# Prompt attention: a third PSUM bank for turned probabilities, one bank for the values of all branches

## What is computed

```
scale = HEAD_DIM ** -0.5
p_c = masked_softmax(jnp.einsum('bqghd,bngd->bghqn', qg, kc) * scale, mask_c)
o_c = jnp.einsum('bghqn,bngd->bqghd', p_c, vc)             # 32 compressed keys
...
p_s = masked_softmax(jnp.einsum('bqghd,bgqkd->bghqk', qg, kg) * scale, mask_s)
o_s = jnp.einsum('bghqk,bgqkd->bqghd', p_s, vg)            # selected keys; here all causal ones
...
p_w = masked_softmax(jnp.einsum('bqghd,blgd->bghql', qg, kw) * scale, mask_w)
o_w = jnp.einsum('bghql,blgd->bqghd', p_w, vw)             # window of 512 keys
o = g[:, :, 0] * o_c + g[:, :, 1] * o_s + g[:, :, 2] * o_w # sigmoid gates per head
```

## Time and profile before

| | |
|---|---|
| median of 3 runs | 1866.81 us (1864.55 to 1866.87) |
| the profiled execution | 1869.97 us, its span 1868.2 us |
| busy, whole span | PE 1665.7, PEld 1275.3, DVE 744.2, ACT 583.4, POOL 379.4 us |
| prompt attention | from 355 to 673 us of the span |

### The profile page before, as it was taken

How to read it: one execution, slowest core, us unless ns; L and a number is a source line. 1 busy time by engine, 2 the same in 40 slices (tenths; PEclk the granted TensorE clock), 3 DMA queues, 4 the chain that set the end, 5 groups by cost and what they waited for, 6 DMA issues and landing times. The chain is left out here.

```text
span 1868.2 us, 27344 instructions
## 1 busy us (share of the span) xinstructions
PE 1665.7 (89%) x11621; PEld 1275.3 (68%) x11621; DVE 744.2 (40%) x1232; ACT 583.4 (31%) x1097; POOL 379.4 (20%) x234
## 2 busy tenths in 40 slices
PE   4899898699989979999999849897999989997698
PEld 4345566466666669999977637784999965554375
DVE  2221111255455456660188734232321444444343
ACT  4001111255444443222245422334330402222221
POOL 1111000011000013322288724111120230000141
PEclk9999898799999999999999968998999989998699
DMA  9222253222111001111111153112000130002621
GB/s 335 67 78 46 84 140 89 73 93 91 46 47 47 2 16 46 46 46 35 27 35 35 57 151 146 57 49 85 24 24 24 35 102 1 23 23 79 228 91 62
DMA packets 120575, 129.93 MB, mean 70 GB/s; under 512 B 16728, under 2 KB 92938, under 8 KB 120326
## 3 DMA queue, kind: packets, MB, share of 16 engines
q1 hardware_dynamic: 120102, 128.08, 21.9%
q0 software_dynamic: 352, 0.10, 0.2%
HBM read 107.05 MB, written 23.18 MB: 70 GB/s over the span
## 5 line engine op out<-in xcount | busy, mean ns | idle before, releaser
L154 PE MATMUL banks<-h_T_high,w_ssd_high 128*128 128x352 f32 x480 | 155.8, 325 | 0.6 <-ACT h_T_high L1353 0.6
L154 PE MATMUL banks<-h_T_rest,w_ssd_high 128*128 128x352 f32 x480 | 156.0, 325 | 0.0
L154 PE MATMUL banks<-h_T_high,w_ssd_rest 128*128 128x352 f32 x480 | 155.2, 323 | 0.0
L154 PE MATMUL banks<-w_attn,h_T 128*128 128x408 f32 (+5 forms) x432 | 148.6, 548 | 0.0
L154 PEld LDWEIGHTS banks<-w_attn,h_T 128*128 128x128 f32 (+1 forms) x432 | 74.3, 183 | 73.2 <-issue 56.0
L1194 DVE TENSOR_REDUCE neg_max_att<-banks 128x1 f32<-128x640 f32 (+7 forms) x128 | 88.9, 701 | 83.2 <-PE banks L154 83.1
L154 PE MATMUL banks<-w_r,h_T 128*128 128x512 f32 (+1 forms) x320 | 117.1, 553 | 0.0
L154 PE MATMUL banks<-out_even_w_high,mix_high 128*128 128x512 f32 (+1 forms) x216 | 88.4, 409 | 16.7 <-DVE out_even_w_rest L2100 12.7
L1133 ACT ACTIVATE p_att<-banks,neg_max_att 128x640 f32<-128x640 f32 (+7 forms) x128 | 89.6, 703 | 26.0 <-DVE neg_max_att L1194 25.0
L1063 PE MATMUL banks<-const_f,p_att 128*128 128x128 f32 x544 | 83.3, 285 | 14.8 <-DVE p_T_att L1199 8.3
L154 PEld LDWEIGHTS banks<-h_T_high,w_ssd_high 128*128 128x128 f32 x480 | 90.2, 188 | 1.3 <-ACT h_T_high L1353 1.2
(11 more groups left out here) (477 smaller groups left out, 3492.1 us busy)
## 6 DMA issues: line engine op xcount, KB each, us to landing
w_mod_late<-in_w_mod_dram SPq DMA_DIRECT2D x8, 2048.0 KB
w_ssd<-in_w_in_even_dram SPq DMA_DIRECT2D x20, 512.0 KB, 3.9
w_mod_rows<-in_w_mod_dram SPq DMA_DIRECT2D x4, 2048.0 KB, 20.1
xin<-in_x_prompt_dram SPq DMA_DIRECT2D x8, 512.0 KB, 7.4
cmp_w<-in_nsa_cmp_w_dram SPq DMA_DIRECT2D x8, 512.0 KB
silu_z_T<-in_state_ssd_dram SPq DMA_DIRECT2D x8, 512.0 KB, 4.3
out_dram<-silu_z_T SPq DMA_DIRECT2D x8, 512.0 KB, 3.5
out_even_x_rows<-in_x_prompt_dram SPq DMA_DIRECT2D x8, 512.0 KB, 3.6
```

The lines of the kernel that those rows point to most:

```text
L154: return nc.tensor.matmul(out, lhsT, rhs, start=start, stop=stop, skip_group_check=True)
```

## The change

The running group number now goes to one of three banks, `4 + g % 3` (banks 4, 5 and 6), and whoever writes such a bank waits for the copy of group g - 3. All value sums go to bank 7, so the first unit of a branch waits until the branch just before it has been scaled. `wait_copied` leaves out waits for negative group numbers. The modulation turn, at group g + 1, waits for the copies of g and g - 2.

```
         def wait_copied(eng, g):
-            eng.wait_ge((copied_dve, copied_act)[engine_of[g]], order_of[g])
+            if g >= 0:
+                eng.wait_ge((copied_dve, copied_act)[engine_of[g]], order_of[g])
...
                 def mod_job(j):
                     g = job_group[j]
                     pe.wait_ge(wm_in, 16 * (j + 1))
-                    wait_copied(pe, g - 2)
-                    mod_products(nc, e, wm, 4 + g % 2).then_inc(t_done, 1)
+                    wait_copied(pe, g - 3)
+                    mod_products(nc, e, wm, 4 + g % 3).then_inc(t_done, 1)
                     if j in (3, 5):
                         wait_copied(pe, g)
-                        wait_copied(pe, g - 1)
-                        mod_turn(nc, e, mrow, 4 + (g + 1) % 2, 0).then_inc(t_done, 1)
+                        wait_copied(pe, g - 2)
+                        mod_turn(nc, e, mrow, 4 + (g + 1) % 3, 0).then_inc(t_done, 1)
...
                     for g, s, blocks in some:
-                        if g >= 2:
-                            wait_copied(pe, g - 2)
+                        if g >= 3:
+                            wait_copied(pe, g - 3)
                         for x, (b, half) in enumerate(blocks):
...
-                            last = nc.tensor.transpose(e.ps[:, 4 + g % 2, x * P:(x + 1) * P], src, e.ident)
+                            last = nc.tensor.transpose(e.ps[:, 4 + g % 3, x * P:(x + 1) * P], src, e.ident)
...
                 def values(n):
                     kind, i, br, hh = units[n]
                     q = 3 * i + (0 if kind == "cmp" else 1 + br)
-                    bank = 6 + q % 2
-                    if q >= 2 and hh == 0:
-                        pe.wait_ge(o_scaled, q - 1)
+                    bank = 7
+                    if q and hh == 0:
+                        pe.wait_ge(o_scaled, q)
...
-                    nc.vector.tensor_tensor(scaled[:, i % 2, kind, :], e.ps[:, 6 + q % 2, :], coefT[:, q % 2, :], ALU.mult).then_inc(o_scaled, 1)
+                    nc.vector.tensor_tensor(scaled[:, i % 2, kind, :], e.ps[:, 7, :], coefT[:, q % 2, :], ALU.mult).then_inc(o_scaled, 1)
```

More of the change, by code:

```diff
@@ L1074, in turn_coef @@
                             c = coef[:, i % 2, kind, h:h + 1].broadcast_to([P, HD])
-                            last = mm(nc, e.ps[half * HD:(half + 1) * HD, 4 + g % 2, hh * P:(hh + 1) * P], c, e.ident, True, True)
+                            last = mm(nc, e.ps[half * HD:(half + 1) * HD, 4 + g % 3, hh * P:(hh + 1) * P], c, e.ident, True, True)
                     last.then_inc(t_done, 1)
@@ L1101, in turn_samples @@
                     pe.wait_ge(o_smp_in, 16 * G)
-                    wait_copied(pe, g - 2)
+                    wait_copied(pe, g - 3)
                     for hh in range(HG):
-                        last = nc.tensor.transpose(e.ps[:, 4 + g % 2, hh * TS:(hh + 1) * TS], A.o_smp[:, hh * P:(hh + 1) * P], e.ident[0:TS, 0:TS])
+                        last = nc.tensor.transpose(e.ps[:, 4 + g % 3, hh * TS:(hh + 1) * TS], A.o_smp[:, hh * P:(hh + 1) * P], e.ident[0:TS, 0:TS])
                     last.then_inc(t_done, 1)
@@ L1138, in copy_group @@
                     act.wait_ge(t_done, g + 1)
-                    nc.scalar.copy(pT[:, s, 0:len(blocks) * P], e.ps[:, 4 + g % 2, 0:len(blocks) * P]).then_inc(copied_act, 1)
+                    nc.scalar.copy(pT[:, s, 0:len(blocks) * P], e.ps[:, 4 + g % 3, 0:len(blocks) * P]).then_inc(copied_act, 1)
                 def copy_coef(i, kind):
@@ L1146, in copy_coef @@
                         act.wait_ge(o_scaled, q - 1)
-                    nc.scalar.copy(coefT[:, q % 2, :], e.ps[:, 4 + g % 2, :]).then_inc(copied_act, 1)
+                    nc.scalar.copy(coefT[:, q % 2, :], e.ps[:, 4 + g % 3, :]).then_inc(copied_act, 1)
                 for n in range(-1, len(units)):
@@ L1164, in _ @@
                             act.wait_ge(gates_saved, 16 * 8)
-                        nc.scalar.copy(mrow[:, j % 2, :], e.ps[:, 4 + g % 2, 0:P]).then_inc(copied_act, 1)
+                        nc.scalar.copy(mrow[:, j % 2, :], e.ps[:, 4 + g % 3, 0:P]).then_inc(copied_act, 1)
             @block.gpsimd
@@ L1198, in copy_group @@
                     dve.wait_ge(t_done, g + 1)
-                    nc.vector.tensor_copy(pT[:, s, 0:len(blocks) * P], e.ps[:, 4 + g % 2, 0:len(blocks) * P]).then_inc(copied_dve, 1)
+                    nc.vector.tensor_copy(pT[:, s, 0:len(blocks) * P], e.ps[:, 4 + g % 3, 0:len(blocks) * P]).then_inc(copied_dve, 1)
                 def close(n):
@@ L1240, in _ @@
                         z = A.oT[:, :, TP:T]
-                        nc.vector.tensor_tensor(z, e.ps[:, 4 + sample_group % 2, 0:HG * TS].rearrange("p (h t) -> p h t", h=HG), z, ALU.mult).then_inc(copied_dve, 1)
+                        nc.vector.tensor_tensor(z, e.ps[:, 4 + sample_group % 3, 0:HG * TS].rearrange("p (h t) -> p h t", h=HG), z, ALU.mult).then_inc(copied_dve, 1)
                     if n in jobs and jobs[n] in (3, 5):
@@ L1244, in _ @@
                         dve.wait_ge(t_done, g + 1)
-                        mod_finish(nc, e, link, 1, jobs[n] // 2 - 1, 4 + g % 2, 0)
+                        mod_finish(nc, e, link, 1, jobs[n] // 2 - 1, 4 + g % 3, 0)
                         dve.sem_inc(copied_dve, 1)
```

## The result

The changed kernel takes 1854.71 us (median of 11 runs, 1852.21 to 1862.38) against 1866.29 (11 runs, 1862.64 to 1868.76) in the same sessions: ratio 0.9946, interval 0.9933 to 0.9959, or 10.1 us less. The ratio agrees with that of the means, 1855.6 against 1865.7 us; the medians alone lie 11.6 us apart. I had forecast 5.4 us less and a range from 1857.5 to 1866.5: the direction was right, the size was not.

A forecast was written before the change was run, and what follows sets the result against it. TensorE was taken as prompt attention's busiest engine, with only idle time to win and the exponentials' loop bounding some passes. Third bank 6.2 us less value bank 0.8 gave 5.4 us: 1866.8 to 1861.4 us, range 1857.5 to 1866.5.

The forecast's parts named there:

- A wait of w on TensorE costs about w + 0.07: Prompt attention, i = 4 to 7: a transpose's bank wait costs its idle time plus 0.07 us of lost overlap with value products.
- passes won in full: Ten bank waits in passes where TensorE is late by itself: 3.37 us of waits plus 0.70 of overlap, 4.07 us won.
- The clock: Removing waits buys no clock, granted 1.00 from 366 to 672 us; falls after 673 us may move the result 1 to 2 us.
- The third bank's gain of 6.2 us: Bank waits removed at i = 4 to 7: 4.07 + 1.81 + 0.34 us; bounds nothing and 14.8 us.
- won in part: Ten waits where TensorE's lateness against the exponentials, 0.13 to 0.42 us, limits the gain: 1.81 us in all.
- The loop: For i >= 4, scores, maxima, exponential, next scores run beside TensorE's order and bound some passes; example passes stay 5.13 us apart.
- The lone value bank: Value products wait for the preceding branch's scaling; of 23 places the first four branches are uncovered, costing 0.8 us, bounds 0.3 and 1.23.
- I take all 32 waits as gone: All transposes' waits for an uncopied PSUM bank, behind 473 us, 12.6 us in total, vanish with the third bank.
- the value bank as the bound: Rival: scaling comes late at the first eleven branches, 10.8 us against 6.2 won, giving 1871.4 us; chance 0.04.
- the waits moved almost everywhere: Rival: waits move to the exponentials, passes won in part give nothing; 2.8 us gained, 1864.0 us; chance 0.22.
- all idle time back: Rival: all TensorE idle time at banks is won, 14.0 us, giving 1852.8 us; chance 0.07.
- no wait for a bank: Rival: the third group waits as long because of the copy's own transposes; only the 0.8 us cost remains, 1867.6 us; chance 0.05.

The follow-up runs named there:

- pad_end: Against the changed kernel: two extra GpSimd additions, into a buffer nobody reads, at the very end of the stage; ratio 0.9982 to the kernel before the change.
- two_then_three: Against the kernel before the change: two turned and two value banks for i = 0 to 3, three turned and one value bank from i = 4; ratio 0.9958.
- one_value_bank: Against the kernel before the change: all value sums in bank 7, turned probabilities still in banks 4 and 5; ratio 1.0017, stage 313.6 us.
- heads_first_chosen: two_then_three's banks, both heads' maxima and exponentials before copies in passes of up to two groups, or three without coefficient or modulation product behind; ratio 0.9908 to the earlier kernel.
- heads_first_some: Against the changed kernel: both maxima and both exponentials before the copies, except in passes with four groups; ratio 0.9913 to the kernel before the change, stage 295.9 us.

## Why the prediction was off

The classes of passes, and so the mechanism, were right. Two terms of the sum were not: the cost of a wait, and the clock, which the sum put at nothing. Either error alone would have left the result inside the range (1866.3 less the stage's 7.75 is 1858.5); the two together took it out.

- *"A wait of w on TensorE costs about w + 0.07"* is the step of the stage's sum that failed. In nine of the ten passes won in full, waits of 0.24, 0.50, 0.56 and 0.63 gave 0.46, 0.72, 0.78 and 0.85: w + 0.22. The tenth gave 0.55 for 0.24. The rows of the pass of the earlier trace rows show where the 0.22 is. Ten transposes without a gap take 1.24 us up to the values, so eight take 0.99 and two take 0.25. The eight ahead of the wait end at 1.09 by the modelled row, 0.10 more, and the two behind it hold TensorE from 500.50 to 500.87, 0.37 us, 0.12 more. I had counted the overlap at the end of one run and not that the last two transposes hold TensorE longer after a wait. The ten passes gave 5.6 us where 4.07 was forecast.
- *The clock, at nothing in the sum, 1 to 2 us either way as chance.* Timed, the change gave 10.1 us and the stage 7.75, so 2.3 us came from outside it; the profiles say 2.6. It went the same way in both timings of after. I had taken for chance what was in part the kernel's; pad_end and two_then_three show that the end of this stage decides on 4 to 5 us behind it. I had named other clock stretches behind 673 us as a sign of being wrong, and they came. That they fell in favour of this change, and not against it, was luck.
- *The third bank's gain of 6.2 us* measured 8.3: by passes 5.6 us for the ten waits won in full (forecast 4.07), 2.3 for the ten won in part (1.81), 0.4 for the one in ScalarE's queue (0.34). The class of nothing won was right, all 11 of them.
- *The loop.* I took it for untouched in passes as in the earlier trace rows. Of the ten won in part, seven came out within 0.01 us of the forecast. The other three all turn 14 blocks in four groups; there a copy of a late-turned group stood ahead of the exponential, and with the wait gone it came earlier. Two gave 0.31 for 0.14 and one 0.44 for 0.36. The lateness was the bound I used, and the bound moved.
- *The lone value bank, 0.8 us*: 0.8 by itself in one_value_bank, and 0.6 net of the third bank by the end of i = 3 in after. The four late branches were the ones foretold, the other 19 stayed covered.
- *"I take all 32 waits as gone"*: three are left, at four groups, with 1.1 us. A fourth group waits with three banks for the first group of its own unit.
- The rivals: the value bank as the bound fell with one_value_bank; the waits moved almost everywhere fell with the passes won in part, which gave 2.3 us and not nothing; all idle time back fell with the 14.0 us that scores now wait; no wait for a bank fell with the bank waits themselves, 12.6 us before and 1.1 after.

What stays open: why the clock falls or doesn't fall in that stretch, why the first low stretch keeps its distance from the stage's end in all four profiles of after, and why one profile of before missed the second. Shown is that a longer end of the stage brings it back, and that a stage 0.3 us shorter without added work had it too.

## What to carry to other kernels

Read a wait against the loop beside it: a third of these bank waits lay in passes where the exponentials bounded, and freeing them moved the wait only. What a further buffer permits can be worth more than what it gives: the order with both maxima and exponentials ahead of the copies cost 60 us with two banks. With three, it took the stage from 305 to 296 us where it was used in passes of at most three groups, and to 293.5 us where those with a further product behind them were left out too. Price an interruption of a run of short transposes above the idle time that the row shows. Read a stage's gain from the stage, pass by pass, since the total moves by some us with where the stage ends, and even the stage carries 1 us of clock in its second pass.

## What the runs showed of the hardware

- An interrupted run of 128 x 128 float32 transposes cost 0.22 us more than the idle time in the rows, whatever the length of the wait (0.24 to 0.63 us), in nine of ten passes.
- 2.5 us of GpSimd work at the end of a stage made the kernel 6.5 us longer (0.9947 to 0.9982); the granted clock 265 to 290 us behind it read 0.80 instead of 1.00, with TensorE equally busy there (23.19 and 23.20 us of 25) but 136 products in it instead of 169.
- Sixteen coefficient products (float32, 64 weight columns, 128 moving columns) took 1.92 us while the granted clock was at its 1.2 GHz level and 1.04 us at 2.4 GHz (heads_first_chosen and heads_first_some).
